# Two transformer blocks on one core: the evacuation of a head's weighted sum is moved behind the next head's division

## The reference

```python
s = q @ k.T * scale + bias            # masked: causal, or a window of 128
p = exp(s - max(s)); p = p / sum(p)   # the division of the weights
o = p @ v                             # the weighted sum
```

## Time and profile before

| | before |
|---|---|
| median of 3 runs | 2107.52 us (2099.63 to 2108.08) |
| the profiled execution | 2097.37 us, its span 2095.5 us |
| TensorE matmuls busy | 1952.5 us, 93% |
| VectorE busy | 1189.8 us, 57% |
| ScalarE busy | 755.4 us, 36% |
| GpSimd busy | 326.5 us, 16% |
| mean granted TensorE clock | 0.977 |

### The profile page before, as it was taken

How to read it: one execution, slowest core, us unless ns; L and a number is a source line. 1 busy time by engine, 2 the same in 40 slices (tenths; PEclk the granted TensorE clock), 3 DMA queues, 4 the chain that set the end, 5 groups by cost and what they waited for, 6 DMA issues and landing times.

```text
span 2095.5 us, 22429 instructions
## 1 busy us (share of the span) xinstructions
PE 1952.5 (93%) x9050; PEld 1606.5 (77%) x9050; DVE 1189.8 (57%) x1858; ACT 755.4 (36%) x1134; POOL 326.5 (16%) x288
## 2 busy tenths in 40 slices
PE   2999999999999999998999999899888889999996
PEld 1788788778888877876888888768777668888884
DVE  6566555576667645567645554665566464333436
ACT  3566522352332234224322222264555342221223
POOL 3232211021111102004000000246222130000002
PEclk9999999999999999999999999999999989999998
DMA  9522266256556424431645422232111122233221
GB/s 307 143 81 61 67 237 242 99 208 226 199 211 210 152 80 181 161 101 41 250 172 200 161 94 87 81 101 86 41 41 41 61 80 93 89 101 100 95 86 41
DMA packets 126120, 267.55 MB, mean 128 GB/s; under 512 B 4463, under 2 KB 33151, under 8 KB 126016
## 3 DMA queue, kind: packets, MB, share of 16 engines
q1 hardware_dynamic: 121056, 248.59, 34.7%
q0 software_dynamic: 4960, 17.53, 2.3%
HBM read 261.84 MB, written 8.45 MB: 129 GB/s over the span
## 4 chain that ended last, share of the span: by engine, by line
PE 78%; DVE 10%; ACT 6%; issue 2%; POOL 1%; DMA 0%; ACTq 0%; DVEq 0%; POOLq 0%
PE ps L584 24%; PE ps L586 24%; PE ps L585 24%; DVE t L1532 2%; ACT t L1134 1%; DVE t L1584 1%; DVE t L1566 1%; PE ps L697 1%; DVE t L1506 1%; DVE t L1523 1%; DVE t L1520 1%; ACT t L1166 1%; PE ps L679 1%; POOL t L2085 1%; PE ps L681 1%
## 5 line engine op out<-in xcount | busy, mean ns | idle before, releaser
L584 PE MATMUL ps<-t 128*128 128x512 f32 (+1 forms) x2584 | 1005.8, 389 | 34.8 <-DVE t L1506 25.3
L585 PE MATMUL ps<-t 128*128 128x512 f32 (+1 forms) x2584 | 997.3, 386 | 0.0
L586 PE MATMUL ps<-t 128*128 128x512 f32 (+1 forms) x2584 | 997.3, 386 | 0.0
L584 PEld LDWEIGHTS ps<-t 128*128 128x128 f32 x2584 | 488.9, 189 | 141.1 <-issue 29.4
L1412 DVE TENSOR_TENSOR t<-t 128x2048 fp32r<-128x2048 f32 x135 | 310.2, 2298 | 464.1 <-ACT t L1041 464.1
L586 PEld LDWEIGHTS ps<-t 128*128 128x128 f32 x2584 | 488.9, 189 | 103.2
L585 PEld LDWEIGHTS ps<-t 128*128 128x128 f32 x2584 | 489.1, 189 | 97.5 <-issue 1.0
L1041 ACT ACTIVATE t<-t 128x2048 fp32r<-128x2048 f32 x135 | 258.1, 1912 | 613.8 <-PE ps L586 609.6
L1421 DVE CUSTOM_DVE_ANT_0 t<-t 128x1024 f32<-128x1024 f32 x160 | 198.5, 1282 | 19.7 <-DMA t<-in_ada_t 12.0
L1469 DVE SCALAR_TENSOR_TENSOR t<-ps,t 128x512 f32<-128x512 f32 x184 | 132.4, 747 | 82.3 <-PE ps L586 74.0
L1532 DVE TENSOR_TENSOR t<-ps,t 64x512 fp32r<-64x512 f32 (+4 forms) x183 | 103.0, 577 | 133.9 <-ACT t L1166 58.4
(11 more groups left out here) (151 smaller groups left out, 1422.1 us busy)
## 6 DMA issues: line engine op xcount, KB each, us to landing
t<-in_ada SPq DMA_DIRECT2D x48, 1024.0 KB, 5.7
t<-in_gate SPq DMA_DIRECT2D x22, 1024.0 KB, 5.1
t<-in_up SPq DMA_DIRECT2D x22, 1024.0 KB, 5.1
t<-in_down SPq DMA_DIRECT2D x22, 1024.0 KB, 5.0
t<-in_w_in SPq DMA_DIRECT2D x17, 1024.0 KB, 5.7
t<-in_w_mlp_in SPq DMA_DIRECT2D x16, 1024.0 KB, 5.4
t<-in_w_mlp_out SPq DMA_DIRECT2D x16, 1024.0 KB, 5.1
t<-in_ada_t POOLq DMA_DIRECT2D x13, 1024.0 KB, 5.8
```

What stands on the lines that cost most here:

```text
L584: pe.matmul(o, wh, xh, start=first, stop=False)
L585: pe.matmul(o, wh, xl, start=False, stop=False)
L586: return pe.matmul(o, wl, xh, start=False, stop=last)
```

## The change

The evacuation of head h's weighted sum becomes a step of its own, `("out", h)`. It stands in the list before the third step of head h + 1, behind the division of head h + 2 and, for causal heads, behind the transposes `("t", h+1, 2)`; the last head's stands at the end of its own steps. As the output of heads 0 to 3 of stage 1 is written over queries in a tile whose other half heads 4 to 7 use, TensorE now waits for it before the scores of those. What the evacuation does is the same.

```diff
@@ attention_steps
         for at, step in enumerate(seq):
             if at == NORM[kind] and nxt:
                 steps.append(("norm", n + 1))
+            if at == 2 and n:
+                steps.append(("out", n - 1))
             if step[0] != "+":
                 steps.append((step[0], n, int(step[1])))
...
             fill(2 if at < extra else (1 if at < quota[n] else 0))
+    steps.append(("out", n_heads - 1))
     for _ in units:
@@ TensorE, score
                 on.wait_ge(d_lo, *hd["kt"])
+                if st == 1 and 4 <= h < 8:
+                    on.wait_ge(d_lo, "out", 1, h - 4)
@@ ScalarE, attention
-                    elif what == "v" and step[2] == 3:
+                    elif what == "out":
```

## The result

The changed kernel takes 2074.95 us (median of 4 runs, 2071.92 to 2076.34), the kernel before 2103.57 us (4 runs, 2097.68 to 2108.08). The ratio is 0.9871, with a 95% interval of 0.9844 to 0.9898: some 28.6 us or 1.3% faster. The profiled execution took 2071.9 us with a span of 2070.1, against 2095.5 before. The 28.6 us hold some scatter of the kernel before, whose time moves with its granted clock: beside experiment 1 its runs at 0.976 to 0.977 took 2096.2 to 2098.5 us and those at 0.971 to 0.973 took 2101.8 to 2108.8, while the changed kernel's four runs all had 0.978 to 0.980.

The account below looks back on a forecast made before the run. In the attention stages TensorE stands idle waiting for VectorE's low half of transposed weights. Gains of 17.5 us in stage 2 and 7.0 in stage 1, together 24.5, off a median of 2107.5 gave 2083 us; range 2072 to 2100.

Parts of the forecast that it names:

- The bound, and what waits: TensorE's costliest wait was transposes waiting for VectorE's low half, 35.3 us in 15 waits; stage 2 had room.
- Plain heads: Heads without GpSimd pieces by the division: t.2 released 1.32 us earlier, next score maximum 0.54 us earlier.
- Heads with pieces: Heads where GpSimd runs weight pieces around the divisions: t.2 2.26 us earlier, next score maximum 1.45 us earlier.
- The prediction's other reading: By the shared-port lock, divisions issued first stay short and delay GpSimd; the sum would not change, ScalarE being later.
- The rival in which GpSimd still holds all of them: Divisions still end with GpSimd's stream, heads with pieces release nothing earlier: about 6 us gained, 2102 us; chance 0.08.
- The sum of stage 2: Gains followed from stall to stall through the second attention stage, claimed to total 17.5 us.
- T2: T and a number: TensorE's stall before that head's first transposes in stage 2; here 2.26 of 2.69 us gained.
- signs of being wrong: Divisions staying at 3.0 us, a new wait before scores or weighted sum, or TensorE's first stalls at T4 remaining.
- The sum of stage 1: First attention stage: three causal-head stalls shrink, less 0.4 us at the end, 7.0 us gained; window heads stall nowhere above 0.6.
- The added wait on TensorE: Before scores of heads 4 to 7 of stage 1, for head h-4's evacuation: costed at nothing, 1.3 us each if uncovered.
- The clock: Granted clock averages 0.96 from 1478 to 1642 us; fewer stalls could return 0 to 5 us, taken as 0.
- The lead is given back at the next step: Rival: the evacuation delays t.3 and the scores, so TensorE meets a new wait; 17 us gained, 2091 us; chance 0.12.

Follow-up runs that it names:

- experiment 1: Only the evacuations behind sliding-window heads moved, causal heads' left in place, against the kernel before: 2102.0 us, ratio 1.0004.
- Causal-only: Only the causal heads' evacuations moved, window heads' left in place, against the kernel before: 2071.34 us, ratio 0.9858.
- 12: Only window heads' evacuations moved, with GpSimd's pieces cut to 32 of 512 columns: 2077.45 us beside 2098.66 for the kernel before, single runs.
- Experiment 8: Causal heads' evacuation put four steps later still than in the change, against the kernel before: 2081.48 us, ratio 0.9905.
- Experiment 4: Causal heads' evacuation split: ScalarE's copy behind its t.3 copy, VectorE's half behind the next score maximum; against the kernel before 2067.66 us, ratio 0.9843.
- (5): Kernel before in its old order, but GpSimd's weight pieces work on 32 of 512 columns: 2076.21 us, ratio 0.9884.
- (9): Kernel before, no evacuation moved, but causal heads' ScalarE and GpSimd weight pieces around the division go behind later steps: 2076.45 us, ratio 0.9879.
- (6): Causal heads' evacuations moved, and GpSimd's pieces cut to 32 of 512 columns, against the kernel before: 2069.32 us, ratio 0.9849.
- (10): Causal heads' evacuation moved and split between ScalarE and VectorE, weight pieces moved as well, against the kernel before: 2062.45 us, ratio 0.981.

## Why the prediction was right, and what in it was off

The forecast was 2083 us in a range of 2072 to 2100, and 2074.95 came, in the lowest eighth of the range. The likeliest case is the one that came, in its mechanism; its own range of 2076 to 2091 was missed by 1 us.

**The bound, and what waits.** Right: TensorE had room in stage 2, and what idled it was the low half of transposed weights. The wait of L1532 for L1172 fell from 24.5 us to 3.2 in 9.

**Plain heads.** t.2 came 1.48 us nearer to the exponential (predicted 1.32) and the next score maximum 0.48 (0.54).

**Heads with pieces.** t.2 came 2.28 us nearer (2.26) and the next score maximum 1.52 (1.45). That the third division ends with the first piece was taken from the nearest row, and the third division's 1.46 us bear it out, as does VectorE's wait of 0.31 us for ScalarE's copy of t.2: ScalarE was the later one. The prediction's other reading, by which all three would be short and GpSimd would wait, did not come: the two that started first kept their length, and the third did not. The rival in which GpSimd still holds all of them falls with that number.

**The sum of stage 2.** The remaining stalls, predicted and found: T2 0.43 and 0.42, T4 0 and 0, T5 0.73 and 0.57, T6 1.22 and 1.19, T12 0.3 and 0, T13 0.41 and 1.02, T14 2.56 and 2.02, T15 2.0 and 2.46. Idle time fell by 17.1 us against 17.5. The sum of the last heads is in part luck: T13, T14 and T15 are off by 0.5 to 0.6 us each, one of them the other way, and a new wait of 0.97 us stands before a score (L684) between T13 and T14. A new wait before a score or a weighted sum was among the prediction's signs of being wrong; it came, but small.

**The sum of stage 1: too large.** 7.0 us were predicted and 3.2 of idle time came. The step that failed is that of the window heads, costed at nothing since they had no stall. Causal-only loses 5.9 us of idle time, so the causal term was off by 1.1. The window heads cost 2.7 of idle time, as experiments 1, 2 and 12 show: the time at which the divisions run moved into a piece of GpSimd. They had no stall, but the prediction didn't ask into what the earlier division would run. The added wait on TensorE shows up nowhere.

**The clock: too small.** It was taken as nothing of 0 to 5 us, "since stalls of 1 to 2 us remain at the end". TensorE's busy time fell by 5.3 us with equal instructions. This and stage 1 cancel nearly, 25.4 us of span against 24.5, and a span of 2070.1 against "near 2071". That they cancel is luck: the two errors have nothing to do with each other. The rest of the 8 us between forecast and median lies in the step from a span to a median. The prediction added the 10 us by which the kernel before's median lay above its profiled execution; the changed kernel's median is 3 us above its own, and before came out at 2103.57 with its fourth run, 6 us above.

**"The lead is given back at the next step".** Not at this place. Experiment 8 shows that the mechanism is real: four steps later the evacuation costs 10 us. Experiment 4 shows a small part of it here, at T6 and T10 and at the scores of the last heads.

**What the prediction didn't ask.** It took the weighted sum as the cause and GpSimd as an aggravation. The experiments show two cures of which each does most of the work alone, here as us of the two stages with the number of the experiment:

| | pieces as they are | pieces short | pieces moved |
|---|---|---|---|
| old order | 354.0 | 332.7 (5) | 332.9 (9) |
| causal heads' evacuation moved | 324.5 (2) | 324.3 (6) | not run |
| moved and split | 317.9 (4) | not run | 315.7 (10) |

The order alone gives 29.5 us. The pieces alone give 21, and behind them the order gives 8.4 more; behind the order short pieces give nothing. Either cure takes VectorE's chain off TensorE's path in most heads with pieces, so the second finds little left. Plain heads tell them apart: T5 keeps its 2.05 us with short pieces in the old order and is 0.55 in the new.

How the clock's share divides is not settled, and it isn't in proportion to the stalls. In stage 2, from its first transposes, causal-only has 12.5 us of idle time and 159.4 busy, the pieces moved in the old order (9) 16.1 and 162.3, and the kernel before 28.9 and 163.5: experiment 9 lost three quarters of the idle time that causal-only lost, and under a third of the busy time.

## What to carry to other kernels

Where a bound engine waits for a short chain on others, list in program order what stands between the chain's first input and its end, and move out what it doesn't need, each engine's half to where that engine is idle; but stop before the next product of the chain, or the wait comes back there. Then look at what else makes the chain's instructions long: a stream of another engine that they run into can be worth nearly as much as the order, and a shift of a microsecond anywhere moves instructions into or out of such a stream. Two cures of one stall are not to be added up.

## What the runs showed of the hardware

A row of short divisions loses far more to a row of GpSimd pieces than the reverse: 3.00 us against 0.88 alone when it starts in the middle of the stream, 1.92 when it starts 0.36 us ahead of it, while three pieces grow from 3.75 to 3.94 us. Only work from SBUF to SBUF was touched. The divisions and the small sum of two SBUF inputs (L1583, 0.78 us against 0.15 with short pieces) were drawn out, while a subtraction that reads PSUM kept its length beside a running piece: the 64x512 low half of the kernel before took 0.68 us beside one (1579.61) and 0.69 with GpSimd idle (1592.20).

With some 20 us of TensorE's idle time gone from the two stages, most of it stalls of 1 to 3 us, its busy time for the same matmuls fell by 5.3 us as well, at a higher granted clock.
